# Wide moving operands for the feed-forward up projections of a decoder step: u stored in eight parts of 130 columns

## What is computed

```python
h = h + 0.5 * post1(SwiGLU_1(pre1(h)))     # feed-forward 1
u = pre_m(h);  [qA kA vA qB kB vB gA gB] = u @ w_in
oA = dilated window attention; oB = stick-breaking attention
h = h + post_m(((sigmoid(gA) * (oA @ p_a)) + (sigmoid(gB) * (oB @ p_b))) @ w_o)
h = h + 0.5 * post2(SwiGLU_2(pre2(h)))     # feed-forward 2

def _half_ffn(h, g_pre, g_post, w_gate, w_up, w_down):
    u = _rms(h, g_pre)
    f = (jax.nn.silu(u @ w_gate) * (u @ w_up)) @ w_down
    return h + 0.5 * _rms(f, g_post)
```

## Time and profile before

| | |
|---|---|
| runs before | 1278.09, 1279.45, 1282.18 us |
| the profiled execution's own time | 1279.07 us |
| its span, first to last instruction | 1277.1 us |
| mean granted TensorE clock | 0.993 of full speed |
| busy share PE / weight loads / DVE / ACT / POOL | 97% / 94% / 39% / 32% / 39% |
| HBM | 96 GB/s over the span |

### The profile page before, as it was taken

One profiled execution on the slowest core, in us unless ns is written; L12 is line 12 of the kernel. 1 busy time (PEld: TensorE's weight loads), 2 busy tenths in 40 slices (PEclk: granted clock), 3 DMA queues, 4 the chain that ended last, 5 costly groups with the idle time before them and its releaser, 6 DMA issues.

```text
span 1277.1 us, 24900 instructions
## 1 busy us (share of the span) xinstructions
PE 1237.4 (97%) x10504; PEld 1206.0 (94%) x10504; DVE 497.6 (39%) x921; ACT 408.4 (32%) x678; POOL 504.3 (39%) x415
## 2 busy tenths in 40 slices
PE   8999999999999999999999889999999999999996
PEld 7999999999998999999988779999999999999995
DVE  4652323321116530455377401848662322321115
ACT  6332122222224242435455322435332122212220
POOL 1343444444454354131413513372243444444451
PEclk9999999999999999999999989999999999999998
DMA  6122222222223223312221465131122222222211
GB/s 234 38 96 99 99 77 87 99 91 91 91 72 119 82 100 109 100 41 94 84 84 68 129 219 198 67 125 41 67 100 99 92 78 93 99 91 91 91 59 67
DMA packets 29075, 123.26 MB, mean 97 GB/s; under 512 B 4442, under 2 KB 10610, under 8 KB 17394
## 3 DMA queue, kind: packets, MB, share of 16 engines
q1 hardware_dynamic: 28994, 122.09, 27.1%
HBM read 115.39 MB, written 6.67 MB: 96 GB/s over the span
## 4 chain that ended last, share of the span: by engine, by line
PE 86%; DVE 5%; ACT 2%; SPq 2%; DMA 1%; DVEq 1%; issue 1%; POOL 1%; POOLq 0%; ACTq 0%
PE bank L1427 26%; PE bank L1428 26%; PE bank L1429 26%; PE bank L1449 2%; DVEq L1061 1%; PE bank L1618 1%; PE bank L1675 1%; PE bank L1660 1%; PE bank L1698 1%; PE bank L1647 1%; SPq L499 1%; PE bank L1684 1%; DVE rinv L1067 1%; POOL w_lo L580 1%; DVE h L1100 1%
## 5 line engine op out<-in xcount | busy, mean ns | idle before, releaser
L580 POOL TENSOR_TENSOR w_lo<-raw,w_hi 128x512 fp32r<-128x512 f32 x368 | 476.0, 1326 | 733.7 <-ACT w_hi L655 547.5
L1427 PE MATMUL bank<-u_hi,w_hi 128*128 128x260 f32 x1952 | 559.6, 287 | 6.3 <-DVE sqb L1154 3.2
L1428 PE MATMUL bank<-u_lo,w_hi 128*128 128x260 f32 x1952 | 551.9, 283 | 0.0
L1429 PE MATMUL bank<-u_hi,w_lo 128*128 128x260 f32 x1952 | 551.7, 283 | 0.0
L1427 PEld LDWEIGHTS bank<-u_hi,w_hi 128*128 128x128 f32 x1952 | 368.4, 189 | 16.2 <-issue 12.0
L1429 PEld LDWEIGHTS bank<-u_hi,w_lo 128*128 128x128 f32 x1952 | 368.5, 189 | 0.0
L1428 PEld LDWEIGHTS bank<-u_lo,w_hi 128*128 128x128 f32 x1952 | 368.5, 189 | 0.0
L655 ACT ACTIVATE w_hi<-raw 128x2048 fp32r<-128x2048 f32 x81 | 154.9, 1912 | 303.9 <-PE bank L1429 303.9
L1427 PE MATMUL bank<-hid_hi,w_hi 128*128 128x260 f32 x704 | 199.3, 283 | 1.0 <-POOL w_lo L580 1.0
L1428 PE MATMUL bank<-hid_lo,w_hi 128*128 128x260 f32 x704 | 198.9, 283 | 0.0
L1429 PE MATMUL bank<-hid_hi,w_lo 128*128 128x260 f32 x704 | 198.8, 282 | 0.0
(11 more groups left out here) (192 smaller groups left out, 1295.6 us busy)
## 6 DMA issues: line engine op xcount, KB each, us to landing
raw<-w_stream SPq DMA_DIRECT2D x84, 1024.0 KB, 4.8
raw<-w_stream SPq DMA_DIRECT2D x8, 768.0 KB, 4.4
e_raw<-w_stream SPq DMA_DIRECT2D x5, 1024.0 KB, 8.3
h<-x_t SPq DMA_DIRECT2D x4, 520.0 KB, 7.2
y_t<-h SPq DMA_DIRECT2D x8, 260.0 KB, 2.3
block<-kb_pool SPq DMA_DIRECT2D x8, 256.0 KB, 3.5
ring<-kb_pool SPq DMA_DIRECT2D x8, 256.0 KB, 3.3
ring<-vb_pool SPq DMA_DIRECT2D x8, 256.0 KB, 5.3
```

What stands on the lines that cost most here:

```text
L580: return pool.tensor_tensor(low[:, a], src[:, a], top[:, a].bitcast(F32), ALU.subtract)
L1427: pe.matmul(out, w, hi_x, start=first, stop=False)
L1428: pe.matmul(out, w, lo_x, start=False, stop=False)
L1429: return pe.matmul(out, v, hi_x, start=False, stop=last)
```

## The change

u becomes one tensor of eight parts of 130 columns, [128, 8, 8, 130]. Group 0's high half-rows are parts 0 and 1, group 1's are 4 and 5; group 0's low half-rows are parts 2 and 7, group 1's are 3 and 6. `product` reads a group as two parts of 130 wherever its operand is u, so the matmuls there stay 260 columns. In the last 16 up chunks of each feed-forward, `wide_item` takes the place of the four `u_item`s of a chunk. For each tile t and each k it issues five matmuls: w_hi with parts 0 to 2 (390 columns), w_hi with parts 3 to 5 (390), w_hi with parts 6 and 7 (260, written to two pieces of a bank that lie 130 columns apart), w_lo with parts 0 and 1 (260), w_lo with parts 4 and 5 (260). Tile t has banks 3t to 3t+2. The low products then lie apart from the high ones, so ACT copies them from PSUM to SBUF (`wide_low`, two instructions of 260 columns), and DVE adds the rest from PSUM (`wide_sum`, two instructions), signals `wide_read[t]`, and works on with 520 columns at a time. Silu now comes after the sum, from SBUF, 520 columns at a time, and stands before `w_hi` of an even slot and after it. `f` shares the place of u and is laid out in the same parts. Before the first wide chunk TensorE waits until all four old banks have been read, and after the last one until both wide sums have been made.

```diff
-    u_hi = perm("u_hi", [P, KD, T], F32R)
-    f = Placed(nc, perm.at)("f", [P, KD, T])
-    u_lo = perm("u_lo", [P, KD, T], F32R)
+    f = Placed(nc, perm.at)("f", [P, 8, KD, HU])
+    u = perm("u", [P, 8, KD, HU], F32R)
...
+HI, LO = (slice(0, 2), slice(4, 6)), (slice(2, 8, 5), slice(3, 7, 3))
...
 TensorE
+            def wide_item(slot, t):
+                a, b, c = banks[:, 3 * t, 0:390], banks[:, 3 * t + 1, 0:390], banks[:, 3 * t + 2, 0:390]
+                by3 = lambda x: x.rearrange("p (a c) -> p a c", a=3)
+                for k in range(KD):
+                    w, v = (tile.rearrange("p (k c) -> p k c", k=KD)[:, k, tile_cols(t)] for tile in w_tiles(slot)[1:])
+                    first, last = k == 0, k == KD - 1
+                    pe.matmul(by3(a), w, u[:, 0:3, k, :], start=first, stop=False)
+                    pe.matmul(by3(b), w, u[:, 3:6, k, :], start=first, stop=False)
+                    pe.matmul(by3(c)[:, 0:3:2, :], w, u[:, 6:8, k, :], start=first, stop=last)
+                    pe.matmul(by3(a)[:, 0:2, :], v, u[:, HI[0], k, :], start=False, stop=last)
+                    mm = pe.matmul(by3(b)[:, 1:3, :], v, u[:, HI[1], k, :], start=False, stop=last)
+                mm.then_inc(wide_full[t], 1)
...
+                pe.wait_ge(lo_made, n0 + UPR + 1)
+                for b in range(4):
+                    pe.wait_ge(read[b], r0 + UPR)
+                for s in range(2):
+                    pe.wait_ge(lo_made, n0 + UPR + s + 1)
+                    for t in range(2):
+                        if s:
+                            pe.wait_ge(wide_read[t], done + UPR + 1)
+                        wide_item(s, t)
-                with pe.Fori(FOLD // 2 + 1, UPS) as i:
+                with pe.Fori(UPR // 2 + 1, UPS) as i:
                     for s in range(2):
                         pe.wait_ge(lo_made, n0 + 1 + s + 2 * i)
-                        for b in range(4):
-                            u_item(s, b, r0 + s + 2 * i)
+                        for t in range(2):
+                            pe.wait_ge(wide_read[t], done + s + 2 * i)
+                            wide_item(s, t)
+                for t in range(2):
+                    pe.wait_ge(wide_read[t], done + 2 * UPS)
 ACT
+            def wide_low(t):
+                for g, low in enumerate((banks[:, 3 * t:3 * t + 3:2, TG:TG + HU], banks[:, 3 * t + 1:3 * t + 3, 0:HU])):
+                    made = act.activation(halves(low_sum[t][:, tg(g)]), low, ACT.Copy)
+                made.then_inc(low_out, 1)
...
+                with act.Fori(UPR // 2, UPS) as i:
                     for s in range(2):
+                        for t in range(2):
+                            act.wait_ge(wide_full[t], done + 1 + s + 2 * i)
+                            wide_low(t)
+                        if s == 0:
+                            act.wait_ge(wide_read[0], done + 1 + 2 * i)
+                            act.activation(sg_wide[:, 0, :], sg_wide[:, 0, :], ACT.Silu).then_inc(gated, 1)
                         act.wait_ge(raw_in[s], raw_at(n0 + 2) + 16 * i)
                         hi_copy(s)
+                        if s == 0:
+                            act.wait_ge(wide_read[1], done + 1 + 2 * i)
+                            act.activation(sg_wide[:, 1, :], sg_wide[:, 1, :], ACT.Silu).then_inc(gated, 1)
 DVE
+            def wide_sum(t, dst, done):
+                for g, top in enumerate((banks[:, 3 * t, 0:TG], banks[:, 3 * t + 1, HU:HU + TG])):
+                    made = dve.tensor_tensor(dst[:, tg(g)], top, low_sum[t][:, tg(g)], ALU.add)
+                made.then_inc(done, 1)
...
+                with dve.Fori(UPR // 2, UPS) as i:
+                    for t in range(2):
+                        dve.wait_ge(low_out, 2 * done + 1 + t + 4 * i)
+                        wide_sum(t, sg_wide[:, t, :], wide_read[t])
+                    for t in range(2):
+                        x = (flat(tmp), flat(sqb))[t]
+                        dve.wait_ge(low_out, 2 * done + 3 + t + 4 * i)
+                        wide_sum(t, x, wide_read[t])
+                        drain()
+                        dve.wait_ge(gated, done + 1 + t + 2 * i)
+                        dve.tensor_tensor(x, x, sg_wide[:, t, :], ALU.mult)
+                        drain()
+                        dve.tensor_copy(top, x)
+                        drain()
+                        dve.tensor_tensor(low, x, top.bitcast(F32), ALU.subtract).then_inc(hid_made, 2)
 u_low, at the first feed-forward: two instructions of 260 columns in place of one of 520
+                    for x in ((g,) if q or again else range(G)):
+                        made = dve.scalar_tensor_tensor(u[:, LO[x], t, :], halves((hn[q] if again else h)[:, t, tg(x)]),
+                                                        gain[:, 2 * q, t:t + 1], u[:, HI[x], t, :].bitcast(F32),
+                                                        ALU.mult, ALU.subtract)
```

More of the change, by code:

```diff
@@ L55 @@
 CHUNKS = 98
[L56 removed]
+R_FFN1, R_QKV, R_PA, R_PB, R_WO, R_FFN2 = 0, 10, 19, 23, 27, 31
 MIX = QKV + 9
@@ L190, in step_program @@
     m_tmp = [tmp[:, 0, :], tmp[:, 1, :], sqb[:, 0, :], sqb[:, 1, :]]
-    psum = [nc.alloc_psum_tensor(f"bank{i}", [P, 512], F32) for i in range(8)]
+    banks = nc.alloc_psum_tensor("banks", [P, 8, 512], F32)
+    psum = [banks[:, i, :] for i in range(8)]
     bank = psum[0:4]
@@ L287, in step_program @@
         stored = sem("stored")
+        wide_full = [sem(f"wide_full{t}") for t in range(2)]
+        wide_read = [sem(f"wide_read{t}") for t in range(2)]
+        low_out = sem("low_out")
+        gated = sem("gated")
         block = ctx.enter_context(nc.Block())
@@ L315, in wait_chunk_used @@
                 else:
-                    eng.wait_ge(full[3], R_FFN1 + 2 * UPS + r + 1)
+                    eng.wait_ge(full[3], R_FFN1 + UPR + r + 1)
             elif n < MIX:
@@ L333, in wait_chunk_used @@
                 else:
-                    eng.wait_ge(full[3], R_FFN2 + 2 * UPS + r + 1)
+                    eng.wait_ge(full[3], R_FFN2 + UPR + r + 1)
         def slot_of(n):
@@ L707, in u_top @@
                 wait_h(q, g, s)
[L708 removed]
                 for t in (2 * s, 2 * s + 1):
[L710 to L711 removed]
+                    if q:
+                        dst, src = u[:, HI[g], t, :], halves(h[:, t, tg(g)])
+                    else:
+                        dst = u[:].rearrange("p (g a) k c -> p g a k c", g=2)[:, :, 0:2, t, :]
+                        src = h[:, t, :].rearrange("p (g a c) -> p g a c", g=2, a=2)
+                    act.activation(dst, src, ACT.Copy, scale=gain[:, 2 * q, t:t + 1]).then_inc(uh_made, 1)
             def u_top_again(q, g, r):
@@ L1183, in ffn_up @@
                     up_gate(q, 1, b)
-                with dve.Fori(FOLD // 2, UPS) as i:
-                    for b in range(4):
-                        dve.wait_ge(full[b], r0 + 2 + 2 * i)
-                        x = tmp[:, b % 2, :]
-                        dve.tensor_tensor(x, sg[:, b, :], out_of(b), ALU.mult).then_inc(read[b], 1)
-                        hidden(i, b, x)
+                for b in range(4):
+                    dve.wait_ge(full[b], r0 + UPR)
+                    x = tmp[:, b % 2, :]
+                    dve.tensor_tensor(x, sg[:, b, :], out_of(b), ALU.mult).then_inc(read[b], 1)
+                    hidden(FOLD // 2, b, x)
+                drain()
+                done = WIDE * (q // 2) - UPR
+                with dve.Fori(UPR // 2, UPS) as i:
[10 more added lines that the diff above has]
+                        drain()
+                        top = hid_hi[:, bass.ds(2 * i + t, 1), :].rearrange("p a c -> p (a c)")
+                        low = hid_lo[:, bass.ds(2 * i + t, 1), :].rearrange("p a c -> p (a c)")
+                        dve.tensor_copy(top, x)
+                        drain()
+                        dve.tensor_tensor(low, x, top.bitcast(F32), ALU.subtract).then_inc(hid_made, 2)
             dve.memset(ones[:], 1.0).then_inc(ones_made, 1)
```

70 lines of the change are left out of this document (41 added, 29 removed).

## The result

1294.22 us, median of four runs (1292.75 to 1295.46), against 1278.77 for the kernel before in the same job: ratio 1.0119 [1.0104, 1.0133]. The change makes the kernel slower by 1.2%. The forecast was 1270.0, the range 1266 to 1284: both missed. The profiled execution took 1295.46 us (span 1293.6, 1.9 outside it), 16.4 more than the profiled one of before. In the later jobs one execution of e8 (2432.84 us) and two of e9 (1351.03 and 6846.88 us) were in a slower state of the chip; the ratios leave them out.

What follows compares the result with a forecast made beforehand. The prediction took TensorE's instruction stream as the bound, with the weight load setting the pace at 260 columns. Wide items -15.1, entry +1.7, exit +4.1 and start +0.2 summed to -9.1 us: 1270.0 us, range 1266 to 1284.

Steps and rivals of the forecast that it cites:

- the 11.5 ns: Each 260-column matmul in the loop takes 119.84 ns, 11.5 more than its columns; the forecast put this on the weight load.
- 165.0 ns for 390 columns: Wide matmuls: longer streaming hides the load, priced from plain fp32 records; 29.5 ns saved per group, -15.1 us.
- Rival B: Wide items: fp32r streams slower per column at full clock, 178.5 ns for 390 columns; +4.7 us, 1283.8; chance 0.13.
- half clock shows no surcharge: At half clock matmuls take 216.7 ns, exactly 260 columns at 1.2 GHz, though each has its weight load.
- "Nothing for" the layout: u and f in parts, and 260-column matmuls reading two parts, were to add no time.
- 9 ns of room under the load: Narrow two-part matmuls of u: slack within 119.84 ns; cover gone, each ns beyond would cost some 4.9 us.
- The clock: At the loop's exit, a 2.05 us wait was to cause no clock fall; a fall would cost a few microseconds.
- entry and exit: TensorE's waits around the wide chunks: 0.84 us per entry and 2.05 per exit, twice each, +1.7 and +4.1 us.
- w_lo ready: In the loop, the weights' low part was to come in time, with 2.6 us of room and no wait of PE.
- ACT and DVE hidden: In the loop, their new copies, Silus and sums per two chunks were to hide beside 22 us of matmuls.
- the third matmul: A rival: its output in two pieces of a bank slows it, or w_lo comes late; beyond 1284; chance 0.06.
- Rival A: Wide items: a fixed surcharge per load stays, 174.0 ns for 390 columns; 5.9 us saved, total 1279.2; chance 0.15.
- rival C: Wide items: loads bank time, so all five matmuls of a group stream; 28.9 us saved, 1256.2; chance 0.04.

Runs made afterwards that it cites:

- e8: e7 with the parts reordered so that every operand of u is one contiguous piece; 1281.51 us, 1.0022 of the kernel before.
- e9: e8 with wide matmuls of 384, 384 and 272 columns and low sums copied in three instructions; 1278.25 us, 0.9983 of the kernel before.
- e10: Kernel before plus test streams at its end: groups of 1560 columns cut four ways, plain fp32, bf16, more fp32r widths; one run, 1556.17 us.
- e1: Kernel before plus streams of 32 fp32r test matmuls at its end, of several widths, in one or more pieces; one run, 1357.12 us.
- e2: Kernel before with u and f laid out in eight parts, no wide items and no added wait; 1290.0 us, 1.0081 of the kernel before.
- e5: Kernel before with only the addresses of u_hi, u_lo and f moved by 8 bytes; 1292.32 us, 1.0099 of the kernel before.
- e6: As e2, but with parts of 52 columns, so a group is five pieces of whole 16-byte lines; 1283.78 us, 1.0041 of the kernel before.
- e7: e3 with the entry and exit waits of TensorE placed later; 1284.11 us, 1.0041 of the kernel before.
- e4: Kernel before plus streams of 64 test matmuls at its end: fp32r widths, pieces and start addresses, and bf16; one run, 1491.28 us.
- e3: Changed kernel with u as [128, k, part, 130], so the 390-column operands are one piece each; 1291.4 us, 1.0096 of the kernel before.

## Why the prediction was wrong

**The mechanism behind the sum fell.** The step that failed is the reading of the 11.5 ns: "I take the weight load as the bound at 260 columns", and from it 165.0 ns for 390 columns "by the nearest row in kind". Plain fp32 was not the nearest row: e10 shows it at two passes of N/2.4 plus 2.5 ns, a rate that fp32r does not have at full clock. Measured: 181.1 and 179.6 (e1: 181). There is a floor, but at 110 to 113 ns (e1: 130 and 200 columns), below the 119.84 that I took the load to be. Per group 727.5 came in place of 689.5; that is 512 x 38 = 19.5 us of the 25.5 between the forecast's -9.1 and the 16.4 of the profiled executions.

Rival B named the mechanism and its price (0.451 ns per column, 178.5; measured 0.453 between 260 and 512 columns). Its evidence for, that no row had fp32r at full clock with another width, was as good as mine. I gave it 0.13 because of the plain fp32 row, and I read "half clock shows no surcharge" as speaking for the load, where it fits both readings alike: a limit of some 1.8 ns per line, if that is what it is, would show at full clock only, since at half clock four columns take 3.3 ns.

**A second step failed: "Nothing for" the layout.** The narrow matmuls were to have 9 ns of room under the load; there was no room, because they were not under it. The step did name what a lost cover would cost, and B said that jumps between parts work the same way, but the range stopped before it. Measured: 1.7 ns each, 10.7 us alone (e2), 4.7 us on the changed kernel's 3360 narrow matmuls (1.4 ns each), and some 2 more inside the wide groups (727.5 against e8's 723.4). By e5 and e6 it is mostly where the pieces begin and end within 16-byte lines, 1.0 of the 1.7 ns, and not the jumps. The number of them was in the diff: 130 columns are 520 bytes.

**The clock.** "The exit's 2.05 us is nearer the first; I take no fall." It fell after the second exit, not after the first, with the same wait before both. I had priced a fall at "a few microseconds"; it was 1.6, in the one execution that was profiled.

**What held.** The sums for entry and exit, though not each link: 0.97 and 0.88 for 0.84, 1.99 and 2.00 for 2.05; 9992 matmuls; w_lo ready over 3 us early and no wait inside the loop; ACT and DVE hidden; the third matmul not slowed by its split output (e1: 121.9 and 121.7; e7 and e8: 119.2 both). The Trainium skill (SBUF — State Buffer, the note on cachelines) says of PSUM that any non-contiguous pattern significantly slows matmuls; two pieces of 130 do not, in e1. The same note speaks of 16-byte cachelines in SBUF and a price for crossing to a new one: as a limit by lines, that agrees with e5 and most rows of e4, but not with plain fp32 (e10), and I had looked at its PSUM half alone. Rival A (174 ns) and rival C fall with e1.

The sum by the measured terms: wide groups +4.4, waits +5.8, clock +1.6, and +4.7 as the rest, for the narrow matmuls. All four are positive. By B a group was to save 2.5 ns even so; e8, with one-piece operands and both waits moved, shows that not even that came. In e10's stream it did: 720.0 against 726.7 for six times 260.

**What stays open.** Why fp32r takes 0.45 ns per column at full clock; every matmul here has a weight load beside it, and no stream ran without, so what the load has to do with it is not shown. Why two and three pieces from column 130, and five of 78, escape the price of the partial line. Why whole-line pieces cost 0.7 ns in the kernel (e6) and nothing in a stream (e4), a group of e8 3.4 ns more than the same group in e10, and six times 260 in e10 7.7 more than in the kernel before. What let the clock fall after one exit of four alike (the changed kernel's and e3's). The fp32r pace also does not grow evenly: e10 has 160 ns for 340, 348 and 352 columns alike, and 170 for 372.

## What to carry to other kernels

A pace that is longer than its columns has at least two readings, a hidden fixed cost and a higher cost per column, and one width can't tell them apart; before widening instructions to hide a fixed cost, time two widths of the same data type. Look at where each moving operand of fp32r begins and ends: with pieces that don't fill 16-byte lines (e2), or tensors that start 8 bytes off (e5), this kernel lost 0.8 and 1.0% with no instruction added. And where a layout is costed at nothing because something hides it, the cover itself must be shown by a row.
